# Staging the gated output projection in X, hraw and yT while they rest, and transposing transfers without a common key

## The reference

```
shift, scale, gate = split(silu(c) @ w_ada + b_ada, 3)        # per sequence, 1024 each
h = rmsnorm(x, norm_g) * (1 + scale) + shift
a_in, a_b, a_c, a_z, b_v, b_g, b_z = split(h @ w_in)          # 7 x 512 columns
y_a = a_b * dwconv3(a_c * a_in) * silu(a_z)
u   = dwconv31(b_v * sigmoid(b_g)) + conv_b_b
y_b = silu(head_layernorm(u)) * silu(b_z)
out = rmsnorm(x + gate * (concat(y_a, y_b) @ w_out), final_g)
```

## Time and profile before

| | us |
|---|---|
| median of 3 runs | 2796.4 |
| lowest and highest run | 2442.5 and 2848.0 |
| profiled execution | 2438.9 |
| its span, slowest core | 2437.3 |
| spans of the 8 cores | 2430.2 to 2437.3 |
| TensorE busy | 2330.8 (96%) |
| DVE busy | 1256.8 (52%) |
| ACT busy | 1056.4 (43%) |
| POOL busy | 563.3 (23%) |

### The profile page before, as it was taken

How to read it: one execution, slowest core, us unless ns; L and a number is a source line. 1 busy time by engine, 2 the same in 40 slices (tenths; PEclk the granted TensorE clock), 3 DMA queues, 4 the chain that set the end, 5 groups by cost and what they waited for, 6 DMA issues and landing times.

```text
span 2437.3 us, 42536 instructions; the slowest of 8 cores (2430.2 to 2437.3 us)
## 1 busy us (share of the span) xinstructions
PE 2330.8 (96%) x13766; PEld 1032.2 (42%) x13766; DVE 1256.8 (52%) x1967; ACT 1056.4 (43%) x1794; POOL 563.3 (23%) x514
## 2 busy tenths in 40 slices
PE   5999999999999999999999799998999989999797
PEld 1444444444444444444444344443444434444343
DVE  0246554555555455545445555455554555554547
ACT  1244345444435544444544335443345434345334
POOL 5114221121122111122212422114222141222302
PEclk7999999999999999999999899998999999999899
DMA  9945655544564554455454654445554455545444
GB/s 235 211 120 132 158 124 144 143 124 114 142 157 120 145 137 119 121 150 146 128 147 127 162 158 119 145 139 149 158 126 142 155 146 141 158 121 162 131 120 176
DMA packets 274566, 350.56 MB, mean 144 GB/s; under 512 B 144392, under 2 KB 217264, under 8 KB 273328
## 3 DMA queue, kind: packets, MB, share of 16 engines
q1 hardware_dynamic: 266736, 340.49, 50.6%
q0 software_dynamic: 7616, 7.34, 2.2%
HBM read 185.73 MB, written 67.13 MB: 104 GB/s over the span
## 4 chain that ended last, share of the span: by engine, by line
PE 83%; DMA 7%; SPq 4%; issue 3%; POOL 2%; DVE 1%; ACT 0%; POOLq 0%; DVEq 0%; ACTq 0%
PE pb L510 53%; PE pb L697 17%; PE pb L582 8%; DMA hraw<-xs 2%; SPq L574 2%; PE pb L494 2%; DMA hraw<-w_out 2%; POOL w_out_sb L460 1%; DMA y<-xb 1%; PE pb L592 1%; PE pb L600 1%; DMA w_out_sb<-w_ada 1%; SPq L294 0%; DVE hT L483 0%; DMA xb<-w_out 0%
## 5 line engine op out<-in xcount | busy, mean ns | idle before, releaser
L510 PE MATMUL pb<-hT,w_in_sb 128*128 128x512 bf16 x6944 | 1505.1, 379 | 0.6 <-PE pb L475 0.2
L510 PEld LDWEIGHTS pb<-hT,w_in_sb 128*128 128x128 bf16 x6944 | 679.4, 98 | 820.8 <-issue 3.1
L697 PE MATMUL pb<-w_out_sb,yT 128*128 128x512 bf16 x2048 | 469.8, 386 | 5.3 <-POOL yT L620 3.2
L660 POOL TENSOR_TENSOR rsE<-msE,mhalf 128x1 f32<-128x1 f32 x128 | 70.2, 548 | 1084.7 <-DVE msE L658 1082.2
L697 PEld LDWEIGHTS pb<-w_out_sb,yT 128*128 128x128 bf16 x2048 | 202.2, 99 | 254.0 <-issue 30.3
L565 DVE SCALAR_TENSOR_TENSOR tp<-t,caT_sb,tp 128x512 f32<-128x512 bf16 x256 | 246.4, 962 | 27.7 <-DVE tp L562 0.5
L542 DVE TENSOR_TENSOR t<-pb,tp 128x512 bf16<-128x512 f32 x128 | 88.9, 695 | 331.5 <-ACT xs L314 301.3
L582 PE MATMUL pb<-X,WC 128*32 128x512 bf16 x4096 | 238.6, 380 | 0.0
L521 DVE SCALAR_TENSOR_TENSOR u<-tp,pb 128x512 bf16<-128x512 f32 x128 | 88.5, 691 | 274.5 <-PE pb L510 262.5
L610 DVE SCALAR_TENSOR_TENSOR pb<-pb,cbs,tp 128x512 f32<-128x512 f32 x128 | 96.7, 756 | 240.1 <-PE pb L600 180.1
L620 POOL TENSOR_TENSOR yT<-tp,gb 128x512 bf16<-128x512 f32 x128 | 151.1, 1181 | 271.4 <-ACT tp L617 271.3
(11 more groups left out here) (87 smaller groups left out, 1353.9 us busy)
## 6 DMA issues: line engine op xcount, KB each, us to landing
xb<-x SPq DMA_DIRECT2D x252, 512.0 KB, 7.4
X<-u SPq DMA_DIRECT2D x512, 135.0 KB, 3.0
y<-xb SPq DMA_DIRECT2D x124, 512.0 KB, 3.5
hraw<-w_out SPq DMA_DIRECT2D x30, 512.0 KB, 4.5
w_in_sb<-w_in POOLq DMA_DIRECT2D x28, 256.0 KB, 16.9
yT<-w_ada SPq DMA_DIRECT2D x6, 1024.0 KB, 11.0
w_out_sb<-w_ada SPq DMA_DIRECT2D x6, 1024.0 KB, 14.8
xb<-w_out SPq DMA_DIRECT2D x10, 512.0 KB, 6.8
```

The source lines that it names most:

```text
L510: T.op("tensor", lambda e, bank=bank, kc=kc: e.matmul(bank[:], lhsT=w_in_sb[:, kc, col0:col0 + 128], rhs=hT[:, kc, :], start=(kc == 0), st ...
L697: T.op("tensor", lambda e, bank=bank, kc=kc, sub=sub, h=h: e.matmul(bank[:], lhsT=yT[:, kc, sub * 128:(sub + 1) * 128], rhs=w_out_sb[:, kc ...
```

## The change

`fold_gate` is taken apart into four functions and no longer has a place in xb for the gate. All eight pieces get a place of their own: four in X, one in hraw's second half (the gate lies in the first), two in the yT that the output stage of the turn has just read, and the last in one xb buffer.

- `begin` is listed after the conv phase of the turn before, ahead of its output stage: the gate and pieces 0 to 4.
- `more` is listed at the start of the turn, ahead of the x loads: pieces 5 and 6.
- `product(0)` to `product(3)` are listed in the GLU stage, one behind each `ln_out`; `last` (the load of piece 7) behind product 3.
- `product(4)` to `product(7)` follow `x_fill`, where all eight were.

`x_fill` and the convolution name the staging keys of X too. The transposes no longer write the hrawf keys; instead each product reads all four hraw keys, and the modulation reads hrawf.

```diff
             for sub in range(4):
                 T.dma("sync", lambda e, sub=sub: e.dma_start_transpose(out=hraw[:, :, sub * 128:(sub + 1) * 128], in_=xs[:, sub, :]),
-                      reads=[("xs", sub)], writes=[("hraw", sub), ("hrawf", 0), ("hrawf", 1)], semkey=("tr", sub))
+                      reads=[("xs", sub)], writes=[("hraw", sub)], semkey=("tr", sub))
...
-        def fold_gate(s):
-
-            gate_bc, gkey = XB.next(pin=True)
-            wb3, wkey3 = XB.next(pin=True)
+        def fold_gate(s, slot):
+
+
+            Xv = X[:].rearrange("p j g n -> p (j g n)").bitcast(F32)
             hv = hraw[:].rearrange("p k n -> p (k n)").bitcast(F32)
+            yv = yT2[slot][:].rearrange("p k n -> p (k n)").bitcast(F32)
             hkeys = [("hraw", sub) for sub in range(4)]
-            stg = [(hv[:, 0:D], [("hrawf", 0)]), (hv[:, D:2 * D], [("hrawf", 1)]), (wb3[:], [wkey3])]
-            T.dma("sync", lambda e: e.dma_start(out=gate_bc[:], in_=gate_d[s:s + 1, :].partition_broadcast(128)),
-                  reads=["gate_d"], writes=[gkey], semkey=("xl", gkey[1]))
+            gate_bc, gkeys = hv[:, 0:D], [("hrawf", 0)]
+            stg = [(Xv[:, n * D:(n + 1) * D], [("Xs", n)]) for n in range(4)]
+            stg.append((hv[:, D:2 * D], [("hrawf", 1)]))
+            stg.append((yv[:, D:2 * D], [("yT", slot, k) for k in range(4, 8)]))
+            stg.append((yv[:, 0:D], [("yT", slot, k) for k in range(4)]))
 
             def load(kc):
-                buf, keys = stg[kc % 3]
-                T.dma("sync", lambda e: e.dma_start(out=buf, in_=wout_d[kc * 128:(kc + 1) * 128, :]),
-                      reads=[], writes=keys + (hkeys if kc < 2 else []), semkey=("fold", kc % 3))
-
-            for kc in range(3):
-                load(kc)
-
-            def finish():
-                for kc in range(8):
-                    buf, keys = stg[kc % 3]
-                    T.op("gpsimd", lambda e, buf=buf, kc=kc: e.tensor_tensor(out=w_out_sb[:, kc, :], in0=buf, in1=gate_bc[:], op=ALU.mult),
-                         reads=keys + [gkey], writes=[("w_out", kc)])
-                    if kc + 3 < 8:
-                        load(kc + 3)
-                XB.unpin(gkey)
-                XB.unpin(wkey3)
-            return finish
+                buf, keys = stg[kc]
+                T.dma("sync", lambda e: e.dma_start(out=buf, in_=wout_d[kc * 128:(kc + 1) * 128, :]), writes=keys, semkey=("fold", kc))
+
+            def begin():
+                T.dma("sync", lambda e: e.dma_start(out=gate_bc, in_=gate_d[s:s + 1, :].partition_broadcast(128)),
+                      reads=["gate_d"], writes=gkeys, semkey=("fold", 8))
+                for kc in range(5):
+                    load(kc)
+
+            def more():
+                load(5)
+                load(6)
+
+            def last():
+                wb, wkey = XB.next(pin=True)
+                stg.append((wb[:], [wkey]))
+                T.dma("sync", lambda e: e.dma_start(out=wb[:], in_=wout_d[7 * 128:8 * 128, :]), writes=[wkey], semkey=("xl", wkey[1]))
+
+            def product(kc):
+                buf, keys = stg[kc]
+                T.op("gpsimd", lambda e: e.tensor_tensor(out=w_out_sb[:, kc, :], in0=buf, in1=gate_bc, op=ALU.mult),
+                     reads=keys + gkeys + hkeys, writes=[("w_out", kc)])
...
-                     reads=[("hraw", sub) for sub in range(4)] + ["gsT", "shT"], writes=[("hT", kc)])
+                     reads=[("hraw", sub) for sub in range(4)] + [("hrawf", kc // 4), "gsT", "shT"], writes=[("hT", kc)])
...
+        Xkeys = ["X"] + [("Xs", n) for n in range(4)]
...
-            T.dma_batch("sync", fns, [("u", slot)], ["X"], "xfill")
+            T.dma_batch("sync", fns, [("u", slot)], Xkeys, "xfill")
...
+            if fold is not None:
+                fold[1]()
             if 1 <= i < ntiles - 1:
                 a_load(i + 1)
...
-                if j == 2 and 2 <= i and tile_first[i - 2]:
-                    fold = fold_gate(tile_seq[i - 2])
+                if fold is not None:
+                    fold[3](j)
+                    if j == 3:
+                        fold[2]()
...
-            if 2 <= i and tile_first[i - 2]:
-                fold()
+            if fold is not None:
+                for kc in range(4, 8):
+                    fold[3](kc)
+                fold = None
...
             hooks, left = conv_phase(i - 1 if 1 <= i <= ntiles else None, i + 1 if i + 1 < ntiles else None)
+            if 1 <= i <= ntiles and tile_first[i - 1]:
+                fold = fold_gate(tile_seq[i - 1], i % 2)
+                fold[0]()
```

More of the change, by code:

```diff
@@ L468, in a_modulate @@
+            def product(kc):
+                buf, keys = stg[kc]
+                T.op("gpsimd", lambda e: e.tensor_tensor(out=w_out_sb[:, kc, :], in0=buf, in1=gate_bc, op=ALU.mult),
+                     reads=keys + gkeys + hkeys, writes=[("w_out", kc)])
+                if kc == 7:
+                    XB.unpin(keys[0])
+            return begin, more, last, product
         def a_modulate(i):
@@ L584, in conv_b @@
                         start=(q == 0), stop=(q == NQ - 1), tile_position=(0, 32 * g)),
-                        reads=[("WC", j), "X"], writes=[bkey], signal=(q == NQ - 1 and g == 3))
+                        reads=[("WC", j)] + Xkeys, writes=[bkey], signal=(q == NQ - 1 and g == 3))
             zb, zkey = sqr.next(pin=True)
@@ L742, in build_nc @@
         a_modulate(0)
-        left = None
+        left, fold = None, None
         for i in range(ntiles + 2):
             cur_ok = i < ntiles
+            if fold is not None:
+                fold[1]()
             if 1 <= i < ntiles - 1:
```

## The result

The changed kernel takes 2375.0 us (median of four runs, 2374.6 to 2376.0), against 2440.4 and 2442.5 us for the kernel before, timed beside it. The ratio is 0.9729, with a 95% interval of 0.9705 to 0.9752. Seven more runs of the kernel before, on the chip of the first experiments, gave 2438.6 to 2441.1.

The account below looks back on a forecast made before the run. TensorE was taken as the bound (83% of the last chain), stalling in five fold turns for w_out. Removing their whole 64.8 us excess from the profiled 2438.9 us gave 2374, stated as 2375 us, range 2366 to 2412.

Parts of the forecast that it names:

- the reserve: Fold turns, transposes before modulation L483: 5 us freed plus 5 us ordinary, 10 us against delays of some 2 us.
- Rival A: GLU stage: DVE scalings and halo copies wait beside POOL products, TensorE for PSUM; 7 us a turn, 2411 us; chance 0.12.
- The whole gain: Five w_out fold turns shrink to an ordinary turn's 71.5 us; their excesses, 64.8 us together, all go.
- Step (1): Gate and pieces 0 to 4 load ahead of the previous turn's output stage; cost 0, cover gone 1 to 4 us.
- Step (3): POOL products: product 3 ends +17.5 to +19.3, product 7 +27 to +30.5; POOL late 0 to 1 us instead of 26.6.
- Steps (4) and (5): Fold turn: x fill after product 3, first transpose late 0 to 0.7 us; piece 7's load costs 0 to 1 us.
- Step (6): Transposes without common key: last lands +39 rather than +44; worth 0 in ordinary turns, 5 us reserve in fold turns.
- Rival B: Fold-turn staging late from a crowded load queue; piece 7 16 us late keeps half the stalls, 2407 us; chance 0.09.
- Rival C: Transposes in flight together hinder one another in 30 turns; 213 us lost, 2588 us; chance 0.06.
- Rival D: Another wait, d loads or a product's guard on hraw, holds modulation L483 just as long; 2439 us; chance 0.05.

## Where the prediction was right and where not, step by step

**The total.** 2375 us forecast, 2375.0 measured. It was set beside the profiled execution, 2438.9 us, and not beside the median of 2796.4; that choice held, since the kernel before took 2440.4 again. The step that failed inside it is the reserve: 10 us was taken as all that the transposes may be late before TensorE loses time, and the runs show a second reserve of 6.6 to 7.7 us behind it. Rival A was priced at the wrong place too. In its sum 5 x 7 is 35, not 36, which changes nothing.

**The whole gain, 64.8 us.** Measured 64.1 in the span. It is the sum of five turn lengths over an ordinary one, and all five are ordinary now. Reading the gain off whole turns carried rest and slow clock together; in the run with only the key removed a rest of 6.79 us again came with 48 matmuls in 12.78 us instead of 10.52.

**Step (1), early loads: 0.** Right in effect, but the loads could as well have been issued at the turn's start.

**Step (3), products: +17.5 to +19.3 and +27 to +30.5.** Measured +19.7 and +28.9. Product 0 took 3.34 us, since it ran into DVE's L678.

**Steps (4) and (5).** The fill began at +19.9 (forecast to +19.3) and took 11.13 us. Piece 7 was issued at +18.3, as its store took 12.2 us and not the 9.44 of the earlier trace rows, within the 2 to 4 us allowed. Together the delays came to 0.1 us at the first transpose, where some 2 were allowed.

**Step (6), the key: 0 in ordinary turns, 5 us of reserve in fold turns.** Right: 0 with the key put back alone, 30 us with it removed alone.

**The reserve, 10 us against delays of 2.** This is the step that failed, though the total did not hang on it. I took a late modulation for a resting TensorE. There are two reserves in series: about 9 us between the last landing and the modulation, as forecast, and 6.6 to 7.7 us more that the modulation may be late before TensorE misses it. The rows of before had it already: a modulation 21.5 us late and a rest of 14.48. With POOL delayed by writes only, the kernel took a modulation 8 us late for under 1 us a turn.

**Rival A, DVE beside POOL.** The collisions came, but short: in the fold turn shown one L678 took 1.61 instead of 1.28 us and the two halo copies 1.35 and 1.01 instead of 0.18, 2.3 us in all where the rival had 11.2, and TensorE saw none of it. The pair of runs with six products and 15 memsets, which differ in the operation too, agrees with the rule behind it: a DVE instruction with two SBUF inputs waits for a GpSimd instruction that reads SBUF (5.41 us for the pair), not for one that only writes (1.62). The Trainium skill says so in "SBUF — State Buffer", section "Who interferes with whom". I priced it at the wrong place, though: it costs once products run beside the short convolution.

**Rival B** would have needed 16 us of delay in the staging; the run with all loads at the start had its first product 6.8 us later, piece 7 10.2 us later, and lost nothing. Its price was too high by the same step: 16 - 10 = 6 us of late modulation is inside the second reserve. **Rival C** did not occur: with four transposes freed the median landing went from 3.1 to 3.3 us over all 120, the longest from 5.0 to 5.9, and ordinary turns stayed at 71.4 us. In the fold turn shown the group took 8.3 us from first issue to last landing, not an estimated 3, for each had to wait for its quarter of xs. **Rival D** did not occur: no product's guard and no d load held the modulation.

## What to carry to other kernels

Find the turns that are longer than their neighbours, subtract, and treat that as the most an edit there can bring; then date every step of the chain from the turn's start and compare it with the hour at which its result is wanted. Edits that only move a date do not add up: each is worth nothing before the edge and its full length behind it, so test one from both sides, put back alone and done alone. Before work is moved to an engine's idle stretch, look at what the other engines do there: the same products cost DVE 2.3 us beside the GLU steps and held up the short convolution, and through it TensorE, when they ran beside that.

## What the runs showed of the hardware that was not expected

A memset of 128x1024 f32 on POOL lasts 0.951 us (median of 115), as estimated from the trace's 312 ns for 128x256 and 204 ns for 128x128, but in a row they stand 1.09 us apart (23 in 25.08): 0.14 us between two of them was not in the estimate. Beside memsets the scaling L573 (one SBUF input, bf16) took up to 1.24 us instead of 0.48, while L576 did not slow.

In the run with nine extra products core 6 ran a whole ordinary turn at a granted clock of 0.83, without a single wait of TensorE:

```profile
256.10:341.20 85.10, 85.10 (x426) 35.03 (x424) 37.74 (x61) 33.01 (x56) 13.42 (x13) 0.83 0.43 113
```

This is neither of the two levels, 1.2 and 2.4 GHz, and no mixture of them shows: cut into pieces of 2 and 6 us, the stretch stands at a steady 0.81 from 175 to 332 us and at 1.00 from 334. It begins 5 us into the first fold turn, behind a rest of 1.5 us. Core 0 had the same rest; its clock stood at 0.72 from 170 to 176 and at 1.00 from there, and its fold turn had further rests of 2.05, 2.44 and 1.21 us, which core 6 did not have at the lower clock. Core 7 showed 0.83 in the same window as core 6. The spans were 2436.5 and 2433.3 us, against 2416 to 2418 for cores 0 to 5. It goes with the spread of that kernel's runs, 2422 to 2440 us, in which other cores were the long ones at other times; what sets it off stays open. It does not belong to the nine products: cores 6 and 7 were 26 to 28 us longer in one run each with all loads at the turn's start and with the last loads ahead.
